# Other places in memory for the weight buffers and the streamed tiles

## What is computed

```python
x = x + hyena_mixer(rmsnorm(x, norm_mix), ...)             # long convolution by FFT, in and out projections
x = x + swiglu(rmsnorm(x, norm_ffn), w_gate, w_up, w_down) # 1024 -> 2816 -> 1024
x = rmsnorm(x, norm_final)
for layer in range(2):
    x = x + (even_mixer, odd_mixer)[layer](rms_norm(x, g_mix[layer]), ...)
    x = x + memory_cross_attention(rms_norm(x, g_xa[layer]), rms_norm(mem, g_mem[layer]), ...)
    x = x + swiglu_2(rms_norm(x, g_ffn[layer]), w_gate[layer], w_up[layer], w_down[layer])
```

## Time and profile before

| | |
|---|---|
| median of 2 runs | 2277.22 us (2275.73 to 2278.72) |
| the profiled execution | 2276.98 us |
| its span, first to last instruction | 2275.1 us |
| mean granted clock of TensorE in it | 0.939 |
| instructions | 22848 |

### The profile page before, as it was taken

One profiled execution on the slowest core, in us unless ns is written; L12 is line 12 of the kernel. 1 busy time (PEld: TensorE's weight loads), 2 busy tenths in 40 slices (PEclk: granted clock), 3 DMA queues, 4 the chain that ended last, 5 costly groups with the idle time before them and its releaser, 6 DMA issues. The chain is left out here.

```text
span 2275.1 us, 22848 instructions
## 1 busy us (share of the span) xinstructions
PE 2113.8 (93%) x8927; PEld 1656.8 (73%) x8927; DVE 1283.7 (56%) x1501; ACT 613.1 (27%) x726; POOL 824.5 (36%) x203
## 2 busy tenths in 40 slices
PE   6888886999999989999978899999999968999999
PEld 5666765788888877555755788888787737888887
DVE  6776787753443375544777644343577768444401
ACT  3553111222222223211222222222122312223211
POOL 3465221344444433200340344444444413444443
PEclk8999988999999999756988999999999979999999
DMA  4122112223322231200230222323322311232232
GB/s 153 56 88 72 39 38 72 77 92 96 107 88 97 94 107 57 75 0 0 93 111 4 89 92 93 108 85 102 97 93 81 123 37 56 93 107 95 88 102 70
DMA packets 169835, 183.62 MB, mean 81 GB/s; under 512 B 4583, under 2 KB 160731, under 8 KB 168996
## 3 DMA queue, kind: packets, MB, share of 16 engines
q1 hardware_dynamic: 166660, 176.42, 24.2%
q10 hardware_dynamic: 3104, 6.21, 0.8%
HBM read 180.52 MB, written 2.10 MB: 80 GB/s over the span
## 5 line engine op out<-in xcount | busy, mean ns | idle before, releaser
L1663 POOL TENSOR_TENSOR w_lo<-w_raw,w_hi 128x2048 fp32r<-128x2048 f32 x167 | 772.9, 4629 | 1363.0 <-ACT w_hi L1363 1363.0
L463 PE MATMUL acc<-a_hi,w_hi 128*128 128x512 f32 x1544 | 613.7, 397 | 33.9 <-POOL w_lo L1663 16.6
L464 PE MATMUL acc<-a_lo,w_hi 128*128 128x512 f32 x1544 | 605.5, 392 | 0.0
L465 PE MATMUL acc<-a_hi,w_lo 128*128 128x512 f32 x1544 | 605.2, 392 | 0.0
L1363 ACT ACTIVATE w_hi<-w_raw 128x2048 fp32r<-128x2048 f32 x167 | 319.8, 1915 | 633.8 <-PE acc L465 629.8
L463 PEld LDWEIGHTS acc<-a_hi,w_hi 128*128 128x128 f32 x1544 | 292.3, 189 | 112.2 <-POOL w_lo L1663 20.6
L464 PEld LDWEIGHTS acc<-a_lo,w_hi 128*128 128x128 f32 x1544 | 292.5, 189 | 63.2 <-issue 2.6
L465 PEld LDWEIGHTS acc<-a_hi,w_lo 128*128 128x128 f32 x1544 | 291.9, 189 | 62.5
L465 PE MATMUL acc<-h_hi,w_lo 128*128 128x512 f32 x528 | 205.4, 389 | 0.0
L463 PE MATMUL acc<-h_hi,w_hi 128*128 128x512 f32 x528 | 205.4, 389 | 0.0
L464 PE MATMUL acc<-h_lo,w_hi 128*128 128x512 f32 x528 | 205.4, 389 | 0.0
(11 more groups left out here) (352 smaller groups left out, 2690.1 us busy)
## 6 DMA issues: line engine op xcount, KB each, us to landing
w_raw<-in_w_gate SPq DMA_DIRECT2D x22, 1024.0 KB, 5.1
w_raw<-in_w_up SPq DMA_DIRECT2D x22, 1024.0 KB, 5.1
w_raw<-in_w_down SPq DMA_DIRECT2D x16, 896.0 KB, 4.6
w_raw<-in_hy_w_in SPq DMA_DIRECT2D x12, 1024.0 KB, 5.0
w_raw<-in_ffn_w_gate SPq DMA_DIRECT2D x11, 1024.0 KB, 5.1
w_raw<-in_ffn_w_up SPq DMA_DIRECT2D x11, 1024.0 KB, 5.1
w_raw<-in_e_w_in SPq DMA_DIRECT2D x10, 1024.0 KB, 5.1
w_raw<-in_xa_wkv SPq DMA_DIRECT2D x8, 1024.0 KB, 5.0
```

Source lines behind the costliest of these rows:

```text
L463: nc.tensor.matmul(o, l_hi, r_hi, start=start, stop=False)
L464: nc.tensor.matmul(o, l_hi, r_lo, start=False, stop=False)
L465: return nc.tensor.matmul(o, l_lo, r_hi, start=False, stop=stop)
L1663: nc.gpsimd.tensor_tensor(w_lo[s][:, :], w_raw[s][:, :], w_hi[s][:, :].bitcast(F32), ALU.subtract)\
```

## The change

It gives other places to the tiles, in bytes within each partition. `past(n)` is the first free place whose distance from the start of w_hi0 is n modulo 2048; `apart(where, n)` is the same from a place within an area. Nothing else differs: after the change every engine has the same list of instructions, in the same order, with the same waits.

| tile | place before | place after | residue from w_hi0's, before and after |
|---|---|---|---|
| w_hi0, w_hi1 | 54272, 62464 | 54272, 62496 | 0, 0 and 0, 32 |
| w_lo0, w_lo1 | 70656, 78848 | 70720, 79360 | 0, 0 and 64, 512 |
| a_hi, a_lo | 87040, 103424 | 87552, 103968 | 0, 0 and 512, 544 |
| tmp0 to sq, start of the region | 119808, 136192 | 120384, 136768 | 0 and 576 |
| h_hi, h_lo | 136192, 181248 | 136768, 182080 | 0, 0 and 576, 832 |
| ye_hi, ye_lo | 177152, 193536 | 179200, 195600 | 0, 0 and 0, 16 |
| xo_hi, xo_lo | 185344, 193536 | 186368, 195712 | 0, 0 and 1024, 128 |
| yo_hi, yo_lo | 161024, 177408 | 163072, 179520 | 256, 256 and 256, 320 |

w_raw, x and alt_r stay where they are. e, o, s, c and m move with the region to 576; y moves with a to 512.

```diff
     w_raw = [at(f"w_raw{s}", [P, BLK]) for s in range(2)]
-    w_hi = [at(f"w_hi{s}", [P, BLK], F32R) for s in range(2)]
-    w_lo = [at(f"w_lo{s}", [P, BLK], F32R) for s in range(2)]
+    origin = base[0]
+    def past(n):
+        return base[0] + (origin + n - base[0]) % 2048
+    w_hi = [at("w_hi0", [P, BLK], F32R)]
+    w_hi.append(at("w_hi1", [P, BLK], F32R, offset=past(32)))
+    base[0] = past(0) + 8192 + 64
+    w_lo = [at("w_lo0", [P, BLK], F32R)]
+    base[0] = past(512)
+    w_lo.append(at("w_lo1", [P, BLK], F32R))
     a_at = base[0]
     a_hi = at("a_hi", [P, KT, T], F32R)
+    base[0] = past(544)
     a_lo = at("a_lo", [P, KT, T], F32R)
+    base[0] = past(576)
...
+    def apart(where, n):
+        return where + (origin + n - where) % 2048
...
     h_hi = put("h_hi", [P, FT, T], F32R)
+    pos[0] = apart(pos[0], 832)
     h_lo = put("h_lo", [P, FT, T], F32R)
...
-    sq_at_q, sq_at_k = pos[0] + 8192, pos[0] + 16384 + 8192
+    pos[0] = apart(pos[0], 0)
+    sq_at_q, sq_at_k = pos[0] + 8192, pos[0] + 16384 + 8192 + 32
     ye_hi = put("ye_hi", [P, KT, T], F32R)
-    ye_lo = put("ye_lo", [P, KT, T], F32R)
+    pos[0] = apart(pos[0], 0)
+    ye_lo = put("ye_lo", [P, 4 + KT * T], F32R)[:, 4:4 + KT * T].rearrange("p (k t) -> p k t", k=KT)
...
+    pos[0] = apart(pos[0], 1024)
     xo_hi = put("xo_hi", [P, XH, T], F32R)
+    pos[0] = apart(pos[0], 128)
     xo_lo = put("xo_lo", [P, XH, T], F32R)
...
+    pos[0] = apart(pos[0], 256)
     yo_hi = put("yo_hi", [P, KT, T], F32R)
+    pos[0] = apart(pos[0], 320)
     yo_lo = put("yo_lo", [P, KT, T], F32R)
```

More of the change, by code:

```diff
@@ L289, in build @@
     y_raw = at("y_raw", [P, 8, HALF], offset=y_lo_at)
-    put, _ = area()
+    put, pos = area()
     h_hi = put("h_hi", [P, FT, T], F32R)
+    pos[0] = apart(pos[0], 832)
     h_lo = put("h_lo", [P, FT, T], F32R)
```

## The result

The changed kernel takes 2307.2 us (median of 2 runs, 2307.16 to 2307.25), against 2277.22 before: a ratio of 1.0132, with a 95% interval of 1.0088 to 1.0175. It is 30 us slower, well clear of the spread of either kernel, though less than 2%. The profiled execution has a span of 2305.4 us where it was 2275.1. The forecast was 2277.0, no change; its first rival, a price per matmul on PE, had said 2308 to 2322.

What follows compares the result with a forecast made beforehand. PE's matmul steps were taken to bound the kernel. The 2275.1 us span plus 1.9 outside it gave 2276.98, plus 0 for PE and feeders: forecast 2277.0 us, 8 in 10 range 2266 to 2324.

Steps and rivals of the forecast that it cites:

- Rival 1: On PE, distances off multiples of 64 cost 0.0049 to 0.0071 us on 6280 matmuls: 31 to 45 us slower; chance 0.31.
- What bounds the kernel: On PE, most time is the start-to-start distance of matmuls times their number; 0.2267 us per 512-column step at full clock.
- The feeders' terms of 0: ScalarE, GpSimd, VectorE and transfers: 0, with ends of -0.11 and +0.56 us a block, hidden in the long stages by slack.
- I therefore take 0 for the pair distance: On PE, distance between streamed tile and loaded slice costs 0; other ends kept were +0.0071 and -0.0133 us.
- The yo row: yo products, 10 steps of 0.227 us each, as with a_hi: distances 0, 256, 512 and so on are equal.
- The 8-column block: Block with 8 weight columns, distances 0 to 224: 13 steps of 0.2315 us, unchanged as k goes on; read as no effect.
- alt_r: Weights 672 bytes off the streamed tile: 8 steps of 0.2338 us, 0.0071 above usual; could mean an odd distance costs that.
- Rival 2: On PE, new distances free some or all of 0.0133 us per step: 2226 us middle, 2175 at the ceiling; chance 0.10.
- Rival 3: On PE, each matmul at 0.237 us and GpSimd's low half beyond its slack: 79 us slower, 2356; chance 0.09.
- no effect: Whole kernel: the new addresses change nothing, 2277.0 us, own range 2268 to 2286; chance 0.50.

Runs made afterwards that it cites:

- others_moved: Kernel before, with PE's pairs left at multiples of 256 and w_raw moved by 32 bytes, tmp, rstd, sumsq, sq by 64: 2275.41 us, ratio 1.0001.
- moved_256: Kernel before, with the tiles moved about as far as in the change, but by multiples of 256 bytes: 2276.35 us, ratio 1.0001.
- w_lo_4: Kernel before, with only both w_lo buffers put 4 bytes off: 2312.92 us, ratio 1.0156.
- both_4: Kernel before, with the streams a and h, high and low parts, put 4 bytes off all weights: 2336.78 us, ratio 1.0262.
- sweep: Kernel before, each streamed family at its own constant distance (a 128, h 192, c, s, e, o, m 160, ye 224, xo 96, yo 64): 2313.42 us, 1.016.
- streams_only: The change with weights back at one residue, a_lo 32 bytes and h 64 bytes off them, ye_lo at 32: 2306.35 us, ratio 1.0131 against before.
- all_32: Kernel before, with all streamed tiles, high and low parts alike, 32 bytes beyond the weights' residue: 2318.69 us, ratio 1.0185.
- fine: Kernel before, with ye 4, h 8, a 16, xo 24 and yo 48 bytes off, the rest at 0: 2306.58 us, ratio 1.0137.
- a_lo_4: Kernel before, with only a_lo and h_lo put 4 bytes off: 2310.13 us, ratio 1.0155.

## Why the prediction was wrong

**What bounds the kernel** was right, and it made the rest readable: the steps of PE are most of the time, and the whole 36.8 us lies in them. The feeders' terms of 0 were right too, by the medians above and by others_moved.

**The step that failed is "I therefore take 0 for the pair distance".** Three rows led to it, and each was read past what it holds.

1. The yo row was read as a test of distance. It tested 256 and multiples of it, and moved_256 shows that these are the very distances at which nothing changes. Its row said that multiples of 256 are alike, not that distance is nothing.
2. The 8-column block was read as "it doesn't change as k goes on", and so as evidence against. But its step is 0.2315 where 0.2267 is usual, and its pairs are at mixed distances. w_lo_4 shows that a triple with one pair apart is long as a whole, so steps with no order in k can still come of distances. The trace after had to look the same by either view: all its tiles are moved by multiples of 32 there, so the block still runs over 0, 32 and so on to 224. What does move it is both_4, where every distance in it is 4 more: 13 steps take 3.08 us, 0.2374 each. So the block was not indifferent to distance. That the distances alone make its usual 0.2315 was not tried by itself, and its first triple, at distance 0, is no shorter than the others.

```profile
934.33 0.40 PE L491 MATMUL acc<-a_lo,w_hi 128*8 128x512 f32 x1
...
937.41 0.40 PE L492 MATMUL acc<-a_hi,w_lo 128*8 128x512 f32 x1
```

3. alt_r was the one clean case, and it was set aside because it "differs in other ways as well". It is 672 bytes off, 160 modulo 256, and its 0.2338 is within 0.4 ns of the 0.2342 that c and s show at 160 in sweep. The row gave the step to 0.2%. Its two peculiarities, a slice loaded eight times running and a far place in memory, were still there in sweep, where it is 64 off and took 0.230. In the change it is at 224 and keeps its 1.87 us, which fits the 233.3 ns of that distance.

**Rival 1** had the sign, the engine and nearly the size: 31 to 45 us, with 30 measured. Its test came out as it said: 15.59 us for the 67 steps (15.5 to 15.7), the h matmul at 394 ns (392 or more), and with h the odd blocks longer than the even (a triple takes 696.8 ns in odd blocks, 688.3 in even, 680.0 before, from the same starts). Its rule was wrong: 64 is no grid, sweep has 2.3 ns at 64, 5.7 at 128 and 6.6 at 192. So its 6280 matmuls were too few (every family of 512-column products took part, the even blocks of h too), while its 0.0049 to 0.0071 was about right (0.0050 in the mean). It also left out what the waits and the clock give back, 7 us here. These two misses pull opposite ways, and that its lower end of 31 us comes so near is in part luck.

**Rival 2** is out for products of 512 columns: no family has a mean step under 226.7 ns at any distance tried. Products of 256 columns, below, do gain, and there it is worth next to nothing. **Rival 3**, 0.237 a step in the long run, is not what the change does, but it is real: both_4 has it, by 4 bytes, and is 60.7 us slower.

**The range**, 2266 to 2324, held the time, but only because rival 1 had been taken into it; the range for "no effect", 2268 to 2286, missed, and its chance of 0.50 was the mistake. Two rows of three at 0.2315 and more, and none off a multiple of 256 at 0.2267, was reason to put rival 1 first. Nor is 2% the least that can be told from none here: the 1.3% was clear with two runs of each kernel.

The Trainium skill, SBUF — State Buffer, "Who interferes with whom", says that PE never waits on anyone. As a statement on other engines it agrees with others_moved, 2275.41 us. Its table also calls PE's two reads, of the streamed operand and of the weights, independent. Read as "their addresses don't matter to each other", as the prediction did, it doesn't hold here: 226.7 ns a step at distance 0 and 237.9 at 4.

## What to carry to other kernels

Put the tiles that PE streams and the slices that it holds at the same residue modulo 256 bytes, each slice too; a kernel that is bound by such steps of 512 columns, with a new slice for each matmul, loses 1 to 5% of each step otherwise (one product here lost nothing), and of the offsets tried the smallest, 4 bytes, cost the most. When you ask whether a quantity matters, list the values at which the trace has it: rows at one value, or at multiples of a period, say nothing, and a single odd case that costs something outweighs them. One pair out of three can be enough to spoil its neighbours, and here half of the move cost nearly as much as the whole.

## What the runs showed of the hardware that was not expected

- The step of a float32r product with 128 weight columns depends on the distance modulo 256 between streamed row and weight slice: 226.7 ns at 0, 228.9 to 237.9 elsewhere, but for one product at 240 that has 226.7 (table above). Distances were tried down to 4 bytes, and the price doesn't grow evenly with them: 4 costs 11.2 ns, 16 costs 5.0, 64 costs 2.3 to 3.7 in the mean, 160 costs 7.5.
- With 256 columns 0 is not the best distance. In streams_only, 84 steps of m at distance 64 take 9.52 us, 0.1133 each; the same 84 before, from 1150.60 to 1160.67, take 0.1199. At 32 (all_32) they take 0.1167. That is the better of two products: in the mean m has 120.6 ns at 0, 116.4 at 64 and 118.1 at 32, and y gains 1.5 ns at 224 (all_32) and 0.2 at 128 (sweep). For the 384 steps with m and y it is at most 384 x 0.0066 = 2.5 us, an estimate, about the 0.1% to which these kernels repeat, and a version with it was not run.

```profile
1161.26 0.28 PE L490 MATMUL acc<-m_hi,w_hi 128*128 128x256 f32 x1
...
1170.78 0.28 PE L490 MATMUL acc<-m_hi,w_hi 128*128 128x256 f32 x1
```

- At one constant distance other than 0 the step can settle at more than one value and keep it through a product or a stage: 0.2333 and 0.229 for h at 64 (streams_only), 0.2266 and 0.2333 at 240 (fine). What picks one is open. It may be why the four times of a_lo_4 lie 13.5 us apart (2301.41 to 2314.90) and the ten of moved_256 only 3.0, but only one run of each was profiled.
- What meets inside the chip when the two addresses lie apart, and why 0 is best for 512 columns and not for 256, stays open. w_lo_4 and a_lo_4 point weakly to the slice held and not to the one being loaded, and don't settle it.
